# Cached-attention pages laid over 32 partitions with four tokens each, scores and value products in that order

## The reference, cut to what matters

```python
kmean = jnp.mean(k_full.astype(jnp.float32), axis=2)          # per block of 256 tokens
gate = jnp.einsum('btcgd,bncd->btcgn', qg.astype(jnp.float32), kmean)
_, sel = lax.top_k(gate, topk)                                # topk = 3 of 16
...
s_sel = jnp.einsum('btcgd,btcgsd->btcgs', qg, k_sel.astype(q.dtype), ...) * scale
p = jax.nn.softmax(jnp.concatenate([s_sel, s_own], axis=-1), axis=-1)
o = (jnp.einsum('btcgs,btcgsd->btcgd', p[..., :nsel], v_sel.astype(jnp.float32))
     + jnp.einsum('btcgs,bscd->btcgd', p[..., nsel:], v_own.astype(jnp.float32)))
```

## Time and profile before

| | us |
|---|---|
| median of the three runs (lowest, highest) | 4021.43 (4019.51, 4022.06) |
| the profiled execution, its own time | 4023.27 |
| its span, first to last instruction | 4021.5 |
| PE busy in the span | 3632.3 |
| DVE, ACT, POOL busy | 1556.0, 650.1, 269.7 |

### The profile page before, as it was taken

How to read it: one execution, slowest core, us unless ns; L and a number is a source line. 1 busy time by engine, 2 the same in 40 slices (tenths; PEclk the granted TensorE clock), 3 DMA queues, 4 the chain that set the end, 5 groups by cost and what they waited for, 6 DMA issues and landing times.

```text
span 4021.5 us, 47871 instructions
## 1 busy us (share of the span) xinstructions
PE 3632.3 (90%) x17832; PEld 2933.9 (73%) x17832; DVE 1556.0 (39%) x2652; ACT 650.1 (16%) x1395; POOL 269.7 (7%) x533
## 2 busy tenths in 40 slices
PE   7999588988888879776899899999999999999997
PEld 5888367777766654554787688888888887888886
DVE  0000455555547864333001433333333334344443
ACT  1000033333322114332000200000000000000003
POOL 0000011010000001344000000000000000000000
PEclk9999899999989879888999999999999999999999
DMA  4222000000012110576421232233322332222221
GB/s 131 73 73 65 2 5 4 3 4 3 3 52 62 52 46 21 157 213 213 118 73 52 64 84 81 78 83 84 84 82 77 82 84 79 83 79 84 82 79 58
DMA packets 452080, 286.82 MB, mean 71 GB/s; under 512 B 22587, under 2 KB 441534, under 8 KB 450160
## 3 DMA queue, kind: packets, MB, share of 16 engines
q1 hardware_dynamic: 437765, 245.89, 21.9%
q0 software_dynamic: 14192, 39.21, 3.3%
HBM read 274.54 MB, written 10.49 MB: 71 GB/s over the span
## 4 chain that ended last, share of the span: by engine, by line
PE 78%; DVE 11%; issue 4%; ACT 2%; DMA 1%; POOL 1%; SPq 1%; POOLq 1%; DVEq 0%; ACTq 0%
PE ps L896 42%; PE ps L527 10%; PE ps L615 7%; PE ps L872 6%; PE ps L756 1%; POOL W L358 1%; PE ps L781 1%; PE ps L606 1%; PE ps L607 1%; PE ps L841 1%; PE ps L880 1%; PE ps L885 1%; PE ps L759 1%; SPq L424 1%; ACT XT L1133 1%
## 5 line engine op out<-in xcount | busy, mean ns | idle before, releaser
L527 PE MATMUL ps<-XT,W 128*128 128x272 f32 (+1 forms) x2496 | 584.6, 397 | 12.8 <-DMA W<-in_w_in_dram 10.6
L527 PEld LDWEIGHTS ps<-XT,W 128*128 128x128 f32 (+1 forms) x2496 | 476.5, 191 | 125.1 <-issue 19.9
L896 PE MATMUL ps<-XT,W 128*128 128x272 f32 x1408 | 338.6, 394 | 17.1 <-ACT XT L1133 17.1
L896 PE MATMUL ps<-XT,SUMS 128*128 128x272 f32 x1408 | 337.0, 392 | 0.0
L896 PEld LDWEIGHTS ps<-XT,W 128*128 128x128 f32 x1408 | 268.4, 191 | 73.1 <-issue 17.5
L896 PEld LDWEIGHTS ps<-XT,SUMS 128*128 128x128 f32 x1408 | 267.5, 190 | 55.1
L1619 DVE TENSOR_TENSOR U2B<-ps,S1B 128x272 f32<-128x272 f32 x76 | 33.5, 441 | 633.0 <-PE ps L896 633.0
L872 PE MATMUL ps<-BIG,W 128*128 128x272 f32 x1024 | 236.7, 394 | 4.5 <-DMA W<-in_w_out_dram 4.5
L872 PEld LDWEIGHTS ps<-BIG,W 128*128 128x128 f32 x1024 | 195.7, 191 | 45.2 <-issue 4.6
L896 PE MATMUL ps<-TD,W 128*128 128x272 f32 x704 | 174.7, 397 | 5.6 <-DVE TD L1576 4.3
L896 PE MATMUL ps<-BIG,W 128*128 128x272 f32 x704 | 172.4, 393 | 2.4 <-ACT CNB L1140 2.4
(11 more groups left out here) (345 smaller groups left out, 4960.4 us busy)
## 6 DMA issues: line engine op xcount, KB each, us to landing
W<-in_w_up_dram SPq DMA_DIRECT2D x176, 512.0 KB, 5.2
W<-in_w_in_dram SPq DMA_DIRECT2D x38, 1024.0 KB, 5.8
W<-in_w_down_dram SPq DMA_DIRECT2D x64, 384.0 KB, 4.4
W<-in_w_down_dram SPq DMA_DIRECT2D x64, 320.0 KB, 3.9
W<-in_cache_k_dram SPq DMA_DIRECT2D x128, 128.0 KB, 3.2
W<-in_cache_k_dram POOLq DMA_DIRECT2D x128, 128.0 KB, 3.3
W<-in_cache_v_dram SPq DMA_DIRECT2D x128, 128.0 KB, 3.1
W<-in_cache_v_dram POOLq DMA_DIRECT2D x128, 128.0 KB, 3.2
```

What stands on the lines that cost most here:

```text
L527: last = nc.tensor.matmul(ps[0:width, 2 * acc + h, 0:HALF], wt[u][:, k, 0:width], XT[:, k, h * HALF:(h + 1) * HALF], start=k == 0, stop=k ...
L896: last = nc.tensor.matmul(ps[:, bank, 0:HALF], weights[:, k * P:(k + 1) * P], x[:, k], start=start and k == 0, stop=k == kc - 1, skip_grou ...
```

## The change

- A page still is one transfer of 128 KB, but now to 32 partitions with four tokens (4 KB) each: page g of a group goes to partitions 32 g to 32 g + 31, and the 1024 columns of a buffer are four token places `s` of 256. Partition 32 g + t, place s holds token 4 t + s of page g.
- The transposes of keys and of probabilities run over s instead of g; their shapes and numbers are the same. Columns of a score row now stand as (s, g, t), so a block of 256 tokens is four pieces of 64 columns, 128 apart. ACT's score copies and DVE's mask follow that; the mask becomes two instructions of 8 x 4 x 64 columns each in place of one.
- The value products run with s outermost, then r, then b, so that consecutive products go to different strips (0, 2, 1, 3 and round again). Both sequences' buffers must have landed before the first of the 16, and both are freed at the end.

```diff
-        ck = cache_k[0].rearrange("g p v d -> g p (v d)")
-        cv = cache_v[0].rearrange("g p v d -> g p (v d)")
+        ck = cache_k[0].rearrange("g (t s) v d -> g t (s v d)", s=4)
+        cv = cache_v[0].rearrange("g (t s) v d -> g t (s v d)", s=4)
...
-                                eng.dma_start(pg[j][:, g], cache[bass.ds(row, 1)].rearrange("a p n -> (a p) n")).then_inc(page_landed[j], 16)
+                                eng.dma_start(pg[j][32 * g:32 * g + 32].rearrange("p s n -> p (s n)"),
+                                              cache[bass.ds(row, 1)].rearrange("a t n -> (a t) n")).then_inc(page_landed[j], 16)
...
-                            for g in range(4):
-                                last = nc.tensor.transpose(ps[:, 2 * b + r, g * P:(g + 1) * P], pg[j][:, g, r * P:(r + 1) * P], ident)
+                            for s in range(4):
+                                last = nc.tensor.transpose(ps[:, 2 * b + r, s * P:(s + 1) * P], pg[j][:, s, r * P:(r + 1) * P], ident)
...
-                    for b in BOTH:
-                        j = (2 * c + b) % 8
+                    pair = [(2 * c + b) % 8 for b in BOTH]
+                    for j in pair:
                         pe.wait_ge(page_landed[j], 64 * (4 * bp + 2 + c // 4) + 64)
+                    for s in range(4):
                         for r in BOTH:
-                            o = 32 * (2 * b + r)
-                            for g in range(4):
-                                last = nc.tensor.matmul(ps[o:o + 32, 7, 0:P], PTD[c % 2][:, g * P + o:g * P + o + 32],
-                                                        pg[j][:, g, r * P:(r + 1) * P], start=(c == 0 and g == 0), stop=False, skip_group_check=True)
-                        last.then_inc(page_free[j], 1)
+                            for b in BOTH:
+                                o = 32 * (2 * b + r)
+                                last = nc.tensor.matmul(ps[o:o + 32, 7, 0:P], PTD[c % 2][:, s * P + o:s * P + o + 32],
+                                                        pg[pair[b]][:, s, r * P:(r + 1) * P], start=(c == 0 and s == 0), stop=False, skip_group_check=True)
+                                if s == 3 and r == 1:
+                                    last.then_inc(page_free[pair[b]], 1)
...
-                        nc.scalar.activation(SCR[:, (2 * c + k) * 256:(2 * c + k + 1) * 256], ps[:, 4 + c % 2, k * 256:(k + 1) * 256], ACT.Copy,
+                        block = lambda x: x.rearrange("p (s k n) -> p s k n", s=4, k=2)[:, :, k]
+                        nc.scalar.activation(block(SCR[:, 512 * c:512 * (c + 1)]), block(ps[:, 4 + c % 2, :]), ACT.Copy,
                                              accum_out=DS[:, 2 * c + k:2 * c + k + 1]).then_inc(S["sc_ev"], 1)
...
-                blocks = SCR[:, 0:PAST_LEN].rearrange("p (n k) -> p n k", k=256)
-                link(nc.vector.tensor_tensor(blocks, blocks, DS[:, 16:32].rearrange("p (n a) -> p n a", a=1).to_broadcast([P, 16, 256]), ALU.add))
+                for k in range(2):
+                    blocks = SCR[:, 0:PAST_LEN].rearrange("p (c s k n) -> p c s k n", c=8, s=4, k=2)[:, :, :, k]
+                    masked = DS[:, 16:32].rearrange("p (c k a b) -> p c k a b", c=8, k=2, a=1)[:, :, k].to_broadcast([P, 8, 4, 64])
+                    l = nc.vector.tensor_tensor(blocks, blocks, masked, ALU.add)
+                link(l)
```

More of the change, by code:

```diff
@@ L268, in hybrid_layer_kernel @@
         W2D = W[:, :, :].rearrange("p a n -> p (a n)")
-        pg = [W2D[:, 1024 * j:1024 * (j + 1)].rearrange("p (g n) -> p g n", n=256) for j in range(8)]
+        pg = [W2D[:, 1024 * j:1024 * (j + 1)].rearrange("p (s n) -> p s n", n=256) for j in range(8)]
         SC_W = PAST_LEN + N_DEC
@@ L846, in _ @@
                         pe.wait_ge(S["ptd_ev"], 9 * bp + c)
-                    for g in range(4):
-                        last = nc.tensor.transpose(ps[:, 4 + c % 2, g * P:(g + 1) * P], SCR[:, (4 * c + g) * P:(4 * c + g + 1) * P], ident)
+                    for s in range(4):
+                        last = nc.tensor.transpose(ps[:, 4 + c % 2, s * P:(s + 1) * P], SCR[:, (4 * c + s) * P:(4 * c + s + 1) * P], ident)
                     last.then_inc(S["ptd_mm"], 1)
```

## The result

The changed kernel takes 4032.84 us in the median of 16 runs (4022.88 to 4038.2); the kernel before, run beside it, 4019.66 (16 runs). The ratio is **1.0033, with a 95% interval of 1.0025 to 1.004**: slower by 13 us, a third of a per cent, where 9 us faster was forecast. The profiled execution took 4035.11 us with a span of 4033.4, 11.9 us more than the span before.

A forecast was written before the change was run, and what follows sets the result against it. POOL's issuing of page transfers in the cached attention was taken as the pace. 4023.27 - 7.4 - 4.0 + 1.5 + 0.6 = 4013.97 us; with the median 1.8 us below the profiled execution, 4012.1, range 4002 to 4036.

The forecast's parts named there:

- The value products: Cached attention, first value group of each pass, strips taken in turn: 15.3 us falls to 7.9, a gain of 7.4 us.
- POOL's steps: POOL's page transfers in the cached attention: 176 on the chain, each instruction 23 ns shorter, 4.0 us less.
- Mask and copies: Cached attention's score mask as two instructions: 0.6 us more over four passes; nothing charged for ACT's score copies.
- Landing: Waits for a page to land, five places in the cached attention: 0.3 us more each, 1.5 us in all.
- rival 1: Cached-attention page loads: transfers become the pace, 1.13 us a pair against POOL's 0.99 step; 24.6 us more, 4041; chance 0.20.
- The test that the prediction named: Key-load stretch: DMA share near 1.00 with landings over 5 us would prove rival 1, under 0.86 refute it.
- Rival 2: Cached-attention page loads: transfers keep pace but the queue grows, 10 us at five places instead of 1.5; 4020.6; chance 0.20.
- The port rule: SBUF partitions 0-63 reach 8 of 16 ports, 64-127 the others; page pair 1.20 us in same half, 0.60 in opposite.

## Why the prediction was wrong

**The value products: right.** 7.9 us less on the chain, 7.4 forecast; 1.99 us at granted clock 0.50, and at 1.00, in the timeline of PE of the kernel after, 1.08 where it was 2.46:

```profile
1679.97 1.08 PE L843 MATMUL ps<-W,BIG 128*32 128x128 f32 x32
```

**POOL's steps: half right.** The instruction fell by more than forecast, from 536 to 489 ns, but the step within a group of four pages only from 0.986 to 0.974 us: 2 us in 176 steps, not 4.0. The working let the 0.45 us between the instructions stand; it is 0.48 now. With 496 ns (half pages over 32) and 502 ns (every second partition) the step is 0.974 too, with 516 ns (every fourth) 0.977, with 518 (64 partitions) and 534 (half pages over 128) 0.980, with 536 ns 0.986: it follows the instruction only in part. What sets it stays open.

**Mask and copies: right.** Eight mask instructions of 2288 ns, 18.0 us of work where it was 17.7, and score copies of 380 ns as before: operands that skip in blocks of 64 columns cost nothing.

**Landing: the step that failed.** The sum had 1.5 us for it, 0.3 at five places; at the four key ends alone it was 35.3 - 13.5 = **21.8 us**. Together: -7.9 - 2 + 0.6 + 21.8 = 12.5, against 11.9 in the spans. That the two agree so closely is partly chance, for the stretches don't one by one. The stretch up to the first value group is 2.0 us shorter though its landing is 1.3 longer, since POOL's first transfer starts 3.2 us earlier (1558.1 in place of 1561.3); the last stretch, from the fourth first value group to the output projection, is 1.2 us longer though its value group is 2.3 shorter: it ran over PE's value products before and runs over POOL after.

One of these differences the traces place. The third pass is some 3 us shorter than its landing and value group would have it, because one of POOL's standstills has left it. Before they are at 1761.64 and, in the third pass, at

```profile
1884.95 3.02 issue
```

and after in the second pass and in the last stretch, at

```profile
1780.59 3.31 issue
1936.94 3.29 issue
```

They stand at fixed places of POOL's sequence: behind its 113th and 217th page in the kernel before, the run with only the strips changed and its half pages, behind the 128th and 244th in every run with the new shapes of page and the old loading of page numbers. So they belong to the program and not to the single execution; what causes them stays open.

What stood behind the 1.5 us was the choice against rival 1. Its row, 9.1 us of engine time for the new page, was set aside as a lonely transfer whose first packet carries a delay, with the remark that POOL's own page got cheaper in the crowd, 7.7 to 7.5. That was the error: two busy queues over 128 partitions say nothing of two over 32, and there the price went the other way, from 7.1 us alone to 9.5. The prediction was right to distrust the row: pages of the new shape that follow each other in one queue cost 7.1, not 9.1. That rival 1 nevertheless had about the price of the pair, 18.1 for 19.0 us, was chance. The test that the prediction named gave its answer plainly: a share of 1.05 and landings over 7 us. Rival 1 decided from 15.8 us for a pair, and the pair is at 19.0.

Its 4041 was 8 us too high all the same; 1.8 us of that are the kernel before, 4019.66 where the prediction had 4021.43. It charged 24.6 us for the growing queue, and 21.8 was found; it charged the landing's 1.5 besides, took POOL's 2 us as lost though POOL still issues at its own pace ahead of a queue that grows, and had 0.5 less for the values. In the softmax the queue empties again: the DMA share is 1.06 from 1739 to 1745 us and 0.00 from 1755 to 1760.

The range, 4002 to 4036, holds the time, and only because it was drawn into the ground between the forecast and rival 1. Rival 2, a grown queue with 2 us at five places, 10 us in all, had the right shape at less than half of the size: the four key ends alone took 21.8 us more.

**The port rule.** The runs show that with both queues at work a page confined to one half of the partitions costs 9.1 to 9.7 us on 32 or 64 neighbours and 7.8 to 7.9 on every second, and one that reaches both halves 6.5 to 7.5. By the Trainium skill (SBUF — State Buffer, "Door 1: The DMA port swizzle") the first reach 8 of 16 ports, the others all 16; the runs agree with that split. Its 27.2 GB/s a port, that is 218 for a half, is an estimate somewhat below the 230 GB/s at which the engines were full, though with pages in both halves by turns, and it does not tell neighbours from every second partition. The prediction had quoted the rule and given it a fifth.

The prediction also had 0.60 us for a pair in opposite halves and "no loss where they never do", worked out from the same section of the Trainium skill. The runs speak against that reading, though none keeps the queues apart. If the pages of the two queues met in one half as often as not, at 1.20 us or 0.60 us a pair, the mean would be 0.90 us (an estimate from the prediction's two prices), inside POOL's step of 0.97; measured were 1.14 us, and with halves changed at every page the price stayed at 9.3 + 9.7 = 19.0 us of engine time a pair, 1.19 us on 16 engines. Unless the queues happened to be in the same half nearly always, opposite halves are not free. Why the price appears only with both queues at work stays open.

## What to carry to other kernels

Before a transfer is given another shape, work out the engine time of a page with all queues at work, and hold the pair against the issue step; a price read from a transfer that runs alone is no price for the stream, in either direction. The 4-KB packets bought nothing here: the price went by where the partitions lie, on one half (9.5 us) or on both (6.5 to 6.9), and not by how many they are. When a change has two parts, time each alone; here the good part alone, the value products round the strips, takes 4012.96 us and the pages' shape gives back three times its gain.

## What the runs showed besides

- SP's DMA instruction depends on the shape at the chip's end: 333 ns over 128 partitions, 316 for 32 neighbours, each the same for whole and half pages, and 467 to 472 for 32 partitions with a step or for 64 neighbours. That alone turned SP into the pace. POOL's went 536 (534 for half pages), 489 (496), and 502 to 518.
- 32 products of 128 columns take 1.08 us when each goes to another strip than the one before, and 2.46 when four in a row go to one.
- A page over 32 neighbours costs 7.1 us of engine time with one queue at work and 9.5 with two; half a page costs 3.7 with two, against 3.5 over 128 partitions.
